# Attention's output norm: root and reciprocal with tokens as rows, spread by plain products

## The reference

```
p = jax.nn.softmax(s, axis=-1).reshape(B, H, 2, Q_BLOCK, S)
p = p[:, :, 0] - lam * p[:, :, 1]
return jnp.einsum('bhqk,bkhe->bqhe', p.astype(v.dtype), v)
...
o = rms_norm(o, subln_g, eps=SUBLN_EPS) * (1.0 - lam_init)
return o.reshape(B, S, D) @ w_o
```

## Time and profile before

| | us |
|---|---|
| median of 3 runs (2075.34 to 2078.84) | 2076.11 |
| the profiled execution | 2074.83 |
| its span, first to last instruction | 2072.8 |
| PE busy / DVE / ACT / POOL | 1907.4 / 811.7 / 764.0 / 776.3 |
| mean granted clock of TensorE, of full speed | 0.972 |

### The profile page before, as it was taken

The page is one execution under the profiler, slowest core; times in us unless marked ns, Lnnn a source line. Parts: engine busy times, 40 slices in busy tenths (PEclk is TensorE's granted clock), DMA queues, the critical chain, the costliest instruction groups (busy, mean ns, idle before and its releaser), DMA issues.

```text
span 2072.8 us, 35505 instructions
## 1 busy us (share of the span) xinstructions
PE 1907.4 (92%) x14984; PEld 1563.6 (75%) x14984; DVE 811.7 (39%) x1297; ACT 764.0 (37%) x1046; POOL 776.3 (37%) x640
## 2 busy tenths in 40 slices
PE   5998988778999999999999799999999999989997
PEld 3666857667788888877677478888888877788876
DVE  5578433456332221017876532222102222423443
ACT  5776333433332222124256532222212323243232
POOL 3444400014434444435431144434445342334452
PEclk8999999998999999999999999999999999999998
DMA  5111100003233332322211023333223221132111
GB/s 173 62 34 61 40 3 4 3 24 103 62 102 101 90 93 97 112 76 92 71 52 42 13 80 91 101 101 96 96 97 97 82 82 41 41 107 82 62 61 62
DMA packets 192357, 149.58 MB, mean 72 GB/s; under 512 B 6890, under 2 KB 190401, under 8 KB 192228
## 3 DMA queue, kind: packets, MB, share of 16 engines
q1 hardware_dynamic: 192228, 147.68, 23.2%
HBM read 145.57 MB, written 2.10 MB: 71 GB/s over the span
## 4 chain that ended last, share of the span: by engine, by line
PE 73%; DVE 11%; issue 7%; ACT 6%; POOL 4%; DMA 0%; DVEq 0%; SPq 0%; ACTq 0%; POOLq 0%
PE psum L2686 20%; PE psum L2688 19%; PE psum L2687 19%; PE psum L2865 4%; POOL w_lo L1213 4%; ACT w_hi L1347 2%; PE psum L3164 1%; PE psum L3177 1%; DVE X_lo L1919 1%; DVE xf L2379 1%; DVE col L2428 1%; DVE tq L2399 1%; PE psum L3274 0%; PE psum L3057 0%; PE psum L3287 0%
## 5 line engine op out<-in xcount | busy, mean ns | idle before, releaser
L1213 POOL TENSOR_TENSOR w_lo<-weight_raw,w_hi 128x256 fp32r<-128x256 f32 (+5 forms) x597 | 731.0, 1257 | 1033.7 <-ACT w_hi L1347 1033.6
L2686 PE MATMUL psum<-X_hi,w_hi 128*128 128x512 f32 x1336 | 548.6, 411 | 33.0 <-DVE X_lo L1919 20.2
L2688 PE MATMUL psum<-X_hi,w_lo 128*128 128x512 f32 x1336 | 525.3, 393 | 0.0
L2687 PE MATMUL psum<-X_lo,w_hi 128*128 128x512 f32 x1336 | 524.8, 393 | 0.0
L1347 ACT ACTIVATE w_hi<-weight_raw 128x2048 fp32r<-128x2048 f32 (+1 forms) x136 | 252.9, 1860 | 294.5 <-PE psum L2688 294.4
L2686 PEld LDWEIGHTS psum<-X_hi,w_hi 128*128 128x128 f32 x1336 | 253.1, 189 | 112.5 <-issue 46.9
L2687 PEld LDWEIGHTS psum<-X_lo,w_hi 128*128 128x128 f32 x1336 | 253.5, 190 | 58.0 <-issue 8.9
L2688 PEld LDWEIGHTS psum<-X_hi,w_lo 128*128 128x128 f32 x1336 | 253.2, 190 | 55.0
L2686 PE MATMUL psum<-w_hi,X_hi 128*128 128x256 f32 x640 | 186.7, 292 | 10.3 <-POOL w_lo L1213 10.2
L2687 PE MATMUL psum<-w_lo,X_hi 128*128 128x256 f32 x640 | 182.3, 285 | 0.0
L2688 PE MATMUL psum<-w_hi,X_lo 128*128 128x256 f32 x640 | 182.1, 285 | 0.0
(11 more groups left out here) (473 smaller groups left out, 2593.1 us busy)
## 6 DMA issues: line engine op xcount, KB each, us to landing
weight_raw<-in_ffn_w_gu SPq DMA_DIRECT2D x88, 512.0 KB, 4.9
weight_raw<-in_l_w_in SPq DMA_DIRECT2D x45, 512.0 KB, 4.5
weight_raw<-in_ffn_w_down SPq DMA_DIRECT2D x40, 512.0 KB, 3.7
weight_raw<-in_kv_w SPq DMA_DIRECT2D x16, 512.0 KB, 4.4
weight_raw<-in_l_w_out SPq DMA_DIRECT2D x16, 512.0 KB, 4.4
weight_raw<-in_rw_w_o SPq DMA_DIRECT2D x12, 512.0 KB, 4.5
weight_raw<-in_rw_w_k SPq DMA_DIRECT2D x8, 512.0 KB, 6.7
weight_raw<-in_rw_w_r SPq DMA_DIRECT2D x8, 512.0 KB, 4.0
```

The lines of the kernel that those rows point to most:

```text
L1213: ins = pool.tensor_tensor(l, r, h.bitcast(F32), ALU.subtract)
L2686: pe.matmul(ps, wh, xh, start=start, stop=False, skip_group_check=True)
L2687: pe.matmul(ps, wh, xl, start=False, stop=False, skip_group_check=True)
L2688: return pe.matmul(ps, wl, xh, start=False, stop=stop, skip_group_check=True)
```

## The change

The 512 x 8 sums of squares are taken with tokens as rows: for each head four plain fp32 products, weights a [128, 128] piece of the squares, one column of ones moving, each into one column of bank 0. DVE adds the scaled epsilon (`lsq`, now [128, 4, 8], no longer preset to 1), ACT takes the root and DVE the reciprocal of those 128 x 32 numbers in place. PE spreads them per head by four plain fp32 products: weights one column of `lsq` repeated 128 times, the 128 x 128 identity moving. The first three heads are spread ahead of `ao` step 0, head k + 3 inside it ahead of tile k. A root on four numbers is placed on ACT in turn 32, ahead of the last head's copy and square. The split into `n_hi` and `n_lo` and the products with `lsq` at L3226 go. ACT's loop of L1782 to L1786 and DVE's of L2463 to L2470 stay; the counts of later waits drop by one.

```diff
-    j.add(("osq",), 0, "A")
+    j.add(("osq",), 0, "D")
...
+        lsq = a_("lsq", [P, TT, HEADS // 2])
...
+                if p == N_UNITS:
+                    act.activation(ybias[:, :], cst[:, 0:TT], ACT.Sqrt)
-            wait_done(act, ("osq",))
-            act.activation(rt[:, :], bank(job_banks(("osq",))[0]), ACT.Sqrt, scale=1.0 / P
-                           ).then_inc(job_a, 1)
-            act.wait_ge(kn_f, 6)
-            act.activation(n_hi[:, :], rt[:, :], ACT.Copy).then_inc(kn_h, 1)
+            wait_job(act, ("osq",))
+            act.activation(lsq[:, :, :], lsq[:, :, :], ACT.Sqrt, scale=1.0 / P).then_inc(o_root, 1)
...
-            link(dve.memset(lsq[:, :, :], 1.0))
...
-            head_inverse(("osq",), 6, n_hi, n_lo)
+            dve.scalar_tensor_tensor(out=lsq[:, :, :], in0=l1s[:, :, :], scalar=1e-5 * P, in1=l1s[:, :, :],
+                                     op0=ALU.mult, op1=ALU.mult).then_inc(o_part, 1)
+            dve.wait_ge(o_part, 1)
+            wait_done(dve, ("osq",))
+            dve.tensor_tensor(lsq[:, :, :], lsq[:, :, :],
+                              bank(job_banks(("osq",))[0], TT * KT).rearrange("p (t k) -> p t k", t=TT), ALU.add
+                              ).then_inc(job_d, 1)
+            dve.wait_ge(o_root, 1)
+            dve.reciprocal(lsq[:, :, :], lsq[:, :, :]).then_inc(o_inv, 1)
...
-                return head_sum(job_banks(("osq",))[0], 1, k, aq[:, k, :], k < 4, k >= 4)
+                for tt in range(TT):
+                    ins = pe.matmul(o[:, KT * tt + k:KT * tt + k + 1], aq[:, k, P * tt:P * tt + P], c_("ones", 1),
+                                    start=True, stop=True, skip_group_check=True)
+                return ins
...
-            pe.wait_ge(kn_l, 6)
-            for k in range(KT):
+            pe.wait_ge(o_inv, 1)
+
+            def output_inverse(k):
                 b = begin(("oinv", k))
-                two(bank(b), heads_r[:, P * k:P * k + P], (n_hi[:, :], n_lo[:, :])).then_inc(job_done, 1)
-            product("ao", XV["attn"])
+                for tt in range(TT):
+                    ins = pe.matmul(psum[:, b, P * tt:P * tt + P], lsq[:, tt, k:k + 1].to_broadcast([P, P]),
+                                    c_("ident"), start=True, stop=True)
+                ins.then_inc(job_done, 1)
+
+            for k in range(3):
+                output_inverse(k)
+            for i in range(4):
+                features(PL.first["ao"] + i, XV["attn"] if i == 0 else None,
+                         parts=(lambda k: output_inverse(k + 3) if k + 3 < KT else None) if i == 0 else None)
```

More of the change, by code:

```diff
@@ L787, in build @@
         PTs = a_("PTs", [P, 2, S])
-        lsq = here(a_.spot[0])("lsq", [P, TT, P])
         tq2 = a_("tq2", [P, 2, S])
@@ L895, in build @@
         sc_max = sem("sc_max")
-        lsq_ready = sem("lsq_ready")
+        o_part, o_root, o_inv = sem("o_part"), sem("o_root"), sem("o_inv")
         half_done, half_out = sem("half_done"), sem("half_out")
@@ L1845, in even_part @@
                     elif what == "inv":
-                        act.wait_ge(kn_f, 7 + i)
+                        act.wait_ge(kn_f, 6 + i)
                         if i:
@@ L1887, in odd_part @@
                                        bias=cst[:, C_EPS5:C_EPS5 + 1], scale=1.0 / P).then_inc(job_a, 1)
-                        act.wait_ge(kn_f, 9)
+                        act.wait_ge(kn_f, 8)
                         act.activation(on_hi[:, :], rt[:, :], ACT.Copy).then_inc(kn_h, 1)
@@ L2532, in even_part @@
                         dve.reciprocal(root, root).then_inc(kn_f, 1)
-                        dve.wait_ge(kn_h, 7 + i)
+                        dve.wait_ge(kn_h, 6 + i)
                         dve.tensor_tensor(en_lo[:, :], root, en_hi[:, :].bitcast(F32), ALU.subtract).then_inc(kn_l, 1)
@@ L2653, in odd_part @@
                     elif what == "inv":
-                        head_inverse(("rvar",), 9, on_hi, on_lo)
+                        head_inverse(("rvar",), 8, on_hi, on_lo)
                     elif what == "rrb":
@@ L3223, in _ @@
                     output_sum(p - N_UNITS + KT - 3)
[L3224 to L3227, removed]
             output_sum(KT - 1).then_inc(job_done, 1)
@@ L3322, in even_part @@
                     elif what in ("gorb", "srb"):
-                        pe.wait_ge(kn_l, 7 if what == "gorb" else 8)
+                        pe.wait_ge(kn_l, 6 if what == "gorb" else 7)
                         b = begin((what, i))
@@ L3399, in odd_part @@
                     elif what == "rrb":
-                        pe.wait_ge(kn_l, 9)
+                        pe.wait_ge(kn_l, 8)
                         b = begin(("rrb", i))
```

## The result

The changed kernel is slower: 2086.41 us, median of 20 runs (2073.24 to 2094.52), against 2075.18 for 20 runs of the kernel before; ratio 1.005, 95% interval 1.0033 to 1.0068. Forecast was 2077.6 and no change. Single executions of either kernel lie up to some 14 us off its median, and the long ones had the lower clock: of the kernel before, an execution of 2063.94 us in a later round shows a mean granted clock of 0.978, one of 2089.08 us 0.963. So the stretch in question is measured from inside, from the first sum of squares of turn 30 on, and the whole times serve as a check. The profiled execution took 2082.76 us (span 2080.8).

A forecast was written before the change was run, and what follows sets the result against it. PE, busy 92% of the span, was taken as the bound. Step 1 starting 0.2 us earlier and a clock loss of 1.7 us gave +1.5 on the median 2076.11: 2077.6 us, range 2074.0 to 2080.6.

The forecast's parts named there:

- The sums in the last turns: Turns 30 to 33 of attention: unpacked one-column sums at 0.11 us a record delay the last sum by 2.1 us.
- E: Last turns: clock falls already during single-column products, half speed until step 0's dense part; +4.9 us, 2081.0; chance 0.10.
- the old hole: Kernel before: PE idle 5.64 us between last sum and spread, then 1.2 GHz; that low clock priced at 3.4 us.
- Root and reciprocal: From the start of the last sum to the start of the spread: 1.9 us instead of 6.7.
- Spread and step 0: Output projection, from first spread to last X_hi: 13.7 us instead of 10.45, heads and tiles alternating on PE.
- Weights of step 1: Ahead of step 1: POOL's low part ends 8.13 us after last X_hi starts; PE waits 3.7 us, net -0.2 us.
- Clock behind the hole: Step 1, after PE's new 3.7 us wait: the clock falls and costs 1.7 us, ends 0 and 3.4.
- rival B: Behind the wait ahead of step 1 the clock holds: -0.2 us, 2075.9; chance 0.20.
- Table load: ACT's 1.28 us load for the root, moved early ahead of the last copy: hidden with 0.5 us to spare.

The follow-up runs named there:

- the run at full clock: Changed kernel with the sums of squares moving 128 columns of ones instead of one; ratio 0.9998 to the kernel before.

## Why the prediction was wrong, and where it was right

**The step that failed** is "The sums in the last turns: +2.1 us". Its count was right, 0.11 us a record at full clock, 3.8 us for turn 30. Its clock was not: I priced 28 products and the values and transposes around them at 2.4 GHz because the earlier trace rows and the turns of the earlier trace rows show it there. The last sum came at 15.82 instead of 10.7. Its upper end, +3.4, was taken from four products of 128 columns at full clock and held nothing for a fall, though the measured term is +7.2.

**The rival that came true** is E, chance 0.10, priced too low. I let it cost 3.4 us ahead of the last X_hi, what the old hole had cost. It cost 26.3 to 34.87, 8.6 us, because 20 us ran at half speed, not 6.8: everything from the values block behind turn 30's sums to the spread of the first heads. Against it I had said that ACT and DVE parts don't slow, which is true, but the PE blocks between them are in line with them; and that one-column products elsewhere stand in dense steps without harm, which is no evidence for a stretch of them.

**Root and reciprocal:** forecast 1.9 us, 2.86 at half clock and 2.16 in the run at full clock. The 3.35 us reciprocal and the splitting did go. **Spread and step 0:** forecast 13.7, 16.2 at low clock, 14.05 at full clock. Repeated weights cost no more than others: 32 records of the first four heads with their two waits in 4.11 us there. **Weights of step 1:** forecast 8.13 us from the last X_hi to POOL's end and a hole of 3.7; the hole was 3.55. **Clock behind the hole:** forecast 1.7 us; from PE's 1195.85 to the marker 12.88 us, 1.8 more than the 11.1 at full clock before. In the second profile with sums left out it was nothing, the clock of the prediction's rival B. **Table load:** hidden.

In sum: last sum +7.2, then -3.8 to the spread, +5.7 to the last X_hi, -0.8 to the start of step 1, +1.8 in it, together +10.1. The forecast was +2.1, -4.8, +3.3, -0.8 and +1.7, +1.5. With 128 moving columns the forecast is met to half a us. The range of 2074.0 to 2080.6 was too narrow, since the rival that broke a condition of every term, the clock, was given one old price instead of its own sum.

The Trainium skill (TensorE: Matmul & The Clock Gate, section Why this matters for your kernels) advises to put small outputs at different column groups so that they run side by side; the trace agrees, since four heads packed take 1.06 us and one alone 1.04, against 3.8 for the same four heads here, and giving this up was also what took the long products out of these turns. The Trainium skill's TensorEngine Tiling (Array Packing), section Instruction Overhead, would have a one-column product cost about 60 cycles. No run here shows that for plain products with 128 x 128 weights: they cost 0.11 us a record at full clock with 1, 16 or 128 columns.

## What to carry to other kernels

Before PE work is priced from a row, ask what clock the row had and whether the change takes away the work that stood before the low stretches: wide products that looked like a cost may be what keeps the rest of a thin stage fast. If a product is bound by its weight load, moving more columns beside the load can be free, as 128 were here (32 records in 3.74 us, 3.64 with 16), and here it turned a loss of 0.5% into none. And when PE is relieved, read which preparation ended last before: a margin of 0.84 us on POOL meant that the next us won would be lost there, until one rounding was moved up.

## What the runs showed of the hardware that I had not expected

PE was busy all of the 3.3 us before the fall (3.30 of 3.30, weight loads too), and the clock fell behind one-column products as it does behind idle time; behind 16 columns as well, not behind 128, in two executions. Three profiles came to turn 30 with the clock at 0.50: the kernel before, and the one with heads 3 to 7 beside step 0, were back at 1.00 within half a us of the first packed products, the changed kernel was not in the 6.83 us of its one-column ones. These are single executions, and why the clock had been low there is open. At the 1.2 GHz level a record bound by its weight load takes 0.21 us instead of 0.11 (3.41 us for 16 records), so that the loads slow down with the clock too.
